# Output stage: head gates multiplied in first, the root's table loaded early, and the query columns repacked 256 wide for the U products

## The reference

```python
z = rmsnorm(x) * (1 + scale1) + shift1          # then one projection, three head groups
oa = gated_head_norm(hgrn2(...), ag, a_norm_g)  # heads of 64
ob = rglru(...) * gelu(by)
oc = gated_head_norm(delta(...), cz, dn_norm_g)
x = x + gt1 * (concat([oa, ob, oc]) @ w_out)
h = rmsnorm(x, norm2_g) * (1 + sc2) + sh2
q = h @ wq                                      # 8 heads of 128
# s1, s2 = the halves of q against 128 keys each; the 16 best pairs are the experts of a token
act = gelu(einsum('thkd,td->thk', u[idx], h))
x = x + gt2 * einsum('thk,thkd->td', softmax(scores) * act, v[idx])

def gated_head_norm(o, z, g):
    y = o * rsqrt(mean(o * o, axis=-1) + EPS)
    return y * g * silu(z)
```

## Time and profile before

| | |
|---|---|
| median of 3 runs | 2415.09 us (2414.5 to 2415.49) |
| the profiled execution | 2413.16 us, span 2411.3 us, mean granted clock 0.953 |
| PE matmuls busy | 2272.0 us (94%), 20740 instructions |
| PE weight loads busy | 2112.7 us (88%) |
| DVE, ACT, POOL busy | 1560.5 us (65%), 1271.9 us (53%), 1180.5 us (49%) |
| U products, PE L460 and L464 | 4096 and 2048 matmuls of 256 columns, mean 281 and 280 ns |
| V products, PE L2646 and L2650 | 4096 and 2048 matmuls of 256 columns, mean 279 and 279 ns |
| a high part on ACT, 128 x 512 (L408) | mean 632 ns |

### The profile page before, as it was taken

The page is one execution under the profiler, slowest core; times in us unless marked ns, Lnnn a source line. Parts: engine busy times, 40 slices in busy tenths (PEclk is TensorE's granted clock), DMA queues, the critical chain, the costliest instruction groups (busy, mean ns, idle before and its releaser), DMA issues. The chain is left out here.

```text
span 2411.3 us, 59210 instructions
## 1 busy us (share of the span) xinstructions
PE 2272.0 (94%) x20740; PEld 2112.7 (88%) x20740; DVE 1560.5 (65%) x3155; ACT 1271.9 (53%) x2423; POOL 1180.5 (49%) x1064
## 2 busy tenths in 40 slices
PE   6987989999999999999979789899999999999998
PEld 4954879999998799999979357899999987999997
DVE  2737756973224968888657466589532268787885
ACT  2540245558556955555536203455675578555554
POOL 0005147884445746566300232688744466565661
PEclk7988889999999999999979679999999999999999
DMA  6466024555553079889534740445555511898992
GB/s 251 169 253 228 3 107 156 176 187 190 189 184 112 0 258 313 282 302 312 178 143 165 264 166 12 142 166 175 191 192 184 189 54 69 283 311 278 312 309 102
DMA packets 123825, 455.58 MB, mean 189 GB/s; under 512 B 13744, under 2 KB 14256, under 8 KB 122544
## 3 DMA queue, kind: packets, MB, share of 16 engines
q1 hardware_dynamic: 105264, 386.80, 44.3%
q0 software_dynamic: 18432, 67.12, 9.9%
HBM read 449.37 MB, written 4.49 MB: 188 GB/s over the span
## 5 line engine op out<-in xcount | busy, mean ns | idle before, releaser
L415 POOL TENSOR_TENSOR parts<-ring,parts 128x512 fp32r<-128x512 f32 x358 | 462.6, 1294 | 283.3 <-ACT parts L408 266.3
L408 ACT ACTIVATE parts<-ring 128x512 fp32r<-128x512 f32 x616 | 386.7, 632 | 369.2 <-PE ps_u L464 285.4
L460 PE MATMUL ps_u<-h_parts,parts 128*128 128x256 f32 x4096 | 569.4, 281 | 1.0 <-ACT parts L408 0.6
L2646 PE MATMUL ps_y<-act_parts,parts 128*128 128x256 f32 x4096 | 562.5, 279 | 0.0
L460 PEld LDWEIGHTS ps_u<-h_parts,parts 128*128 128x128 f32 x4096 | 518.2, 189 | 3.5 <-ACT parts L408 2.2
L2646 PEld LDWEIGHTS ps_y<-act_parts,parts 128*128 128x128 f32 x4096 | 515.0, 188 | 0.9 <-ACT parts L2586 0.7
L415 DVE TENSOR_TENSOR parts<-ring,parts 128x512 fp32r<-128x512 f32 x258 | 178.6, 695 | 390.0 <-ACT parts L408 366.0
L2695 POOL TENSOR_TENSOR act_parts<-big,act_parts 128x256 fp32r<-128x256 f32 x256 | 245.5, 959 | 305.7 <-ACT act_parts L2675 305.7
L464 PE MATMUL ps_u<-h_parts,parts 128*128 128x256 f32 x2048 | 324.1, 280 | 1.1 <-DVE parts L415 0.8
L2650 PE MATMUL ps_y<-act_parts,parts 128*128 128x256 f32 x2048 | 322.2, 279 | 0.0
L464 PEld LDWEIGHTS ps_u<-h_parts,parts 128*128 128x128 f32 x2048 | 279.2, 190 | 2.0 <-DVE parts L415 1.2
(11 more groups left out here) (394 smaller groups left out, 3109.0 us busy)
## 6 DMA issues: line engine op xcount, KB each, us to landing
ring<-in_stream SPq DMA_DIRECT2D x522, 512.0 KB, 3.8
more_ring<-in_stream SPq DMA_DIRECT2D x126, 512.0 KB, 3.5
extra_ring<-in_stream SPq DMA_DIRECT2D x48, 512.0 KB, 5.4
big<-in_stream SPq DMA_DIRECT2D x16, 512.0 KB, 12.0
out_state_out<-big SPq DMA_DIRECT2D x2, 1440.0 KB, 8.4
big<-in_state SPq DMA_DIRECT2D x2, 1280.0 KB, 10.7
big<-in_mixc SPq DMA_DIRECT2D x2, 1024.0 KB, 8.2
big<-in_spots SPq DMA_DIRECT2D x2, 1024.0 KB, 5.4
```

The lines of the kernel that those rows point to most:

```text
L408: eng.activation(m.parts[:, q % PARTS, 0, :], half_tile(m, t, half), ACT.Copy).then_inc(s["hi_ready"], 1)
L415: eng.tensor_tensor(m.parts[:, q % PARTS, 1, :], half_tile(m, t, half), m.parts[:, q % PARTS, 0, :].bitcast(F32), ALU.subtract).then_inc(m ...
L460: pe.matmul(out, hi[:, k, :], hr[:, side, kk, 0:tokens], start=(kk + side == 0), stop=False)
L2646: pe.matmul(ps[:, half * KD // 2 + k, :], hi[:, k, :], act_parts[:, j % AHEAD, side, :], start=False, stop=False)
```

## The change

Three edits, all in the output stage.

1. The gates are multiplied into `m.mixed` before the norm: two instructions for tiles 0 and 1, one of 128 x 864 for tiles 5 to 7. The norm's `scalar_tensor_tensor` is then the last step of a column.
2. A Sqrt of one element makes ScalarE load the root's table before the sums are there. For that the order on ScalarE and VectorE changes: only column part 0 stands ahead of the root, the others behind it.
3. `h_parts` is now interleaved, column by column, hi and lo side by side. For the U products the first 256 tokens of the second norm's output are split once more, into a `narrow` view on the same memory: column k at 512k, its low part 256 further on. Column k may be written when query product 2k+1 has been done, since it covers the wide columns up to k alone.

```diff
@@ output_block, ScalarE
-            for i in range(READY):
-                high(i)
-                mixed_high(i)
+            high(0)
+            mixed_high(0)
+            act.activation(tmp[:, 0, 0:1], m.eps, ACT.Sqrt).then_inc(s["root_loaded"], 1)
             act.wait_ge(s["sums_ready"], 1)
             act.activation(norm, ps[0:12, 4, 0:NT], ACT.Sqrt, bias=m.eps[0:12, :], scale=1.0 / HD).then_inc(s["root_ready"], 1)
+            for i in range(1, READY):
+                mixed_high(i)
+                high(i)
...
+            def again_high(k):
+                act.wait_ge(s["parts_used"], OUT_Q + 2 * k + 2)
+                act.activation(narrow[:, 0, k, :], m.h[:, k, 0:NP], ACT.Copy).then_inc(s["u_hi"], 1)
+
+            again_high(0)
+            again_high(1)
             for q in range(OUT_Q + KD, ALL_Q):
                 high(q)
+                if q % 2:
+                    again_high((q - OUT_Q - 5) // 2)
+            again_high(KD - 2)
+            again_high(KD - 1)
             for h in COPY_ACT:
                 wait_head(act, h)
@@ output_block, VectorE
-            for i in range(READY):
-                mixed_low(i)
+            mixed_low(0)
+            v.wait_ge(s["squares_ready"], 2)
+            for n, t in enumerate(tiles[:2]):
+                v.tensor_tensor(m.mixed[:, t, :], m.mixed[:, t, :], m.zact[:, 6 + t, :], ALU.mult).then_inc(s["gated"], 1)
             v.wait_ge(s["root_ready"], 1)
             v.reciprocal(norm, norm).then_inc(s["inverse"], 1)
...
+            v.tensor_tensor(m.mixed[:, 5:8, :], m.mixed[:, 5:8, :], m.zact[:, 11:14, :], ALU.mult).then_inc(s["gated"], 1)
+            for i in range(1, READY):
+                mixed_low(i)
+            v.wait_ge(s["gated"], 3)
             for n, t in enumerate(tiles):
...
                 v.scalar_tensor_tensor(m.mixed[:, t, :], m.mixed[:, t, :], g, ps[:, spread_bank[n], 0:NT],
-                                       ALU.mult, ALU.mult).then_inc(s["spread_read"], 1)
+                                       ALU.mult, ALU.mult).then_inc(s["normed"], 1)
                 if n:
-                    gated(n - 1)
-                if n > 1:
-                    mixed_low(READY + n - 2)
-            gated(len(tiles) - 1)
-            mixed_low(KD - 2)
+                    mixed_low(READY + n - 1)
             mixed_low(KD - 1)
...
+            for k in range(KD):
+                v.wait_ge(s["u_hi"], k + 1)
+                v.tensor_tensor(narrow[:, 1, k, :], m.h[:, k, 0:NP], narrow[:, 0, k, :].bitcast(F32), ALU.subtract).then_inc(
+                    s["u_lo"], 1)
             for h in COPY_DVE:
@@ build
-            with nc.sbuf_tensor("h_parts", [P, 2, KD, NT], F32R) as hr:
-                output_block(nc, m, l, hr, stream, small_out, state_out)
-                experts_block(nc, m, l, hr, stream, spots_in)
+            with nc.sbuf_tensor("h_parts", [P, KD * 2 * NT], F32R) as parts:
+                wide = parts.rearrange("p (k s t) -> p s k t", s=2, t=NT)
+                narrow = parts[:, 0:KD * 2 * NP].rearrange("p (k s t) -> p s k t", s=2, t=NP)
+                output_block(nc, m, l, wide, narrow, stream, small_out, state_out)
+                experts_block(nc, m, l, narrow, stream, spots_in)
```

More of the change, by code:

```diff
@@ L1979, in _, with output_block @@
             new_state(4)
-def output_block(nc, m, l, hr, stream, small_out, state_out):
-    names = ("step squares_ready sums_ready root_ready inverse spread spread_read normed out_ready x_ready squares2 sums2 "
-             "root2 h_ready hi_ready lo_ready parts_used mix_hi mix_lo h_hi h_lo query_ready query_out outs_saved states_saved")
+def output_block(nc, m, l, hr, narrow, stream, small_out, state_out):
+    names = ("step squares_ready sums_ready root_ready inverse spread normed out_ready x_ready squares2 sums2 "
+             "root2 h_ready hi_ready lo_ready parts_used mix_hi mix_lo h_hi h_lo u_hi u_lo gated root_loaded query_ready query_out outs_saved states_saved")
     tiles = (0, 1, 5, 6, 7)
@@ L2091, in column_low @@
                 v.tensor_tensor(hr[:, 1, k, :], m.h[:, k, :], hr[:, 0, k, :].bitcast(F32), ALU.subtract).then_inc(s["h_lo"], 1)
-            for i in range(READY):
-                mixed_low(i)
+            mixed_low(0)
+            v.wait_ge(s["squares_ready"], 2)
+            for n, t in enumerate(tiles[:2]):
+                v.tensor_tensor(m.mixed[:, t, :], m.mixed[:, t, :], m.zact[:, 6 + t, :], ALU.mult).then_inc(s["gated"], 1)
             v.wait_ge(s["root_ready"], 1)
             v.reciprocal(norm, norm).then_inc(s["inverse"], 1)
-            def gated(n):
-                t = tiles[n]
-                gate = m.zact[:, 6 + t, :] if t < 2 else m.zact[:, 11 + t - 5, :]
-                v.wait_ge(s["spread_read"], n + 1)
-                v.tensor_tensor(m.mixed[:, t, :], m.mixed[:, t, :], gate, ALU.mult).then_inc(s["normed"], 1)
+            v.tensor_tensor(m.mixed[:, 5:8, :], m.mixed[:, 5:8, :], m.zact[:, 11:14, :], ALU.mult).then_inc(s["gated"], 1)
+            for i in range(1, READY):
+                mixed_low(i)
+            v.wait_ge(s["gated"], 3)
             for n, t in enumerate(tiles):
@@ L2134, in _ @@
                 v.tensor_copy(m.query[:, h, :], ps[:, h, 0:NT])
-            v.wait_ge(s["h_lo"], KD)
+            v.wait_ge(s["u_lo"], KD)
         @block.tensor
@@ L2179, in _ @@
             out_product(0, 2, 3)
-            pe.wait_ge(s["spread_read"], 1)
+            pe.wait_ge(s["normed"], 1)
             spread_norm(4)
```

## The result

The changed kernel took 2424.38 us (median of 6 runs, 2422.72 to 2425.98) against 2414.8 us for the kernel before, measured beside it: ratio 1.0037, 95% interval 1.0023 to 1.0050. The forecast was 2427. The profiled execution took 2425.98 us (span 2424.1, mean granted clock 0.948), against a span of 2411.3 before.

A forecast was written before the change was run, and what follows sets the result against it. TensorE's matmuls, busy 94% of the span, bound the kernel. Head +2.0 and +1.5, its clock +2.6, ends +3.7, one fall there +1.8, U 0: +11.6 us, on the 2415.09 median about 2427; range 2413 to 2431.

The forecast's parts named there:

- order of the head, both layers: Output stage's head: late low part 1 delays product 1 and the spreads; +2.0 us layer 0, +1.5 layer 1.
- clock in the head, layer 0, layer 1: Behind the head's longer stop the clock falls in both layers; layer 0 as before, 0, layer 1 +2.6 us.
- longer stop at the ends: Output stage's end: the last column's split and copies follow the last query product; +1.85 us a layer, +3.7 in all.
- clock behind the ends: After the longer stop before the scores, one clock fall in the two layers; +1.8 us, bounds 0 and 5.
- U's beat: U stage: halves stay at 1.413 us despite the repack; 0, bounds -6.9 and +3.4 us.
- GpSimd in the head: GpSimd works beside the reciprocal, then the gate holds it up; a reciprocal blocking it was the +3.2 us high end, dropped.
- The rule of the Trainium skill: VectorE instructions with at most one SBUF input, outside two-port modes, do not contend with GpSimd; removed the head's +3.2 us.
- The note on cachelines: U's reads: only stride inside a read costs; both layouts are read contiguously, so the repack gains nothing.
- rival 2: U halves go to 1.400 us but clock falls come as forecast; +4.7 us, 2419.8; chance 16%.

The follow-up runs named there:

- g2: e1 with 9 fp32 matmuls to an unused bank between output products 0 and 1, both layers; 2418.7 us, ratio 1.0011.
- h1: e2 with 3 fp32 matmuls in TensorE's stop at the output stage's end, on a bank already copied out; 2415.2 us, ratio 0.9993.
- e2: The kernel before with only the repacking (second split into 256-wide columns), without the head edits; 2414.91 us, ratio 1.0002.
- g1: e1 with VectorE's wide gate moved behind low parts 1 and 2; 2417.74 us, ratio 1.0010.
- e1: The kernel before with only the head edits (gates first, early root table), without the repacking; 2422.09 us, ratio 1.0029.
- e3: The kernel before with h_parts interleaved, high and low parts side by side, 288 wide each, no second split; 2413.04 us, ratio 0.9987.
- g4: e3's layout plus another head order that puts nothing ahead of low part 1; 2404.77 us, ratio 0.9951 against the kernel before.
- g3: The changed kernel with its packed query columns 2176 bytes apart instead of 2048; 2426.13 us in one run.
- h2: g4 with e3's layout undone: g4's head order on the kernel before's layout; 2408.57 us, ratio 0.9972.
- e4: The repack alone, packed 256 wide, columns 1024 bytes apart, but high and low parts 9216 bytes apart; 2417.45 us, ratio 1.0011.

## Why the prediction came out, term by term

The time was right within 3 us, but two terms were wrong by about as much as each other, with opposite signs. That they cancelled is luck; the range held because both lay within the bounds that were kept.

| term | predicted | measured | from |
|---|---|---|---|
| order of the head, both layers | +2.0, +1.5 | +1.7, +1.7 | g2 less 0.93, against 74.55 |
| clock in the head, layer 0, layer 1 | 0, +2.6 | +1.2, +4.4 | after less 1.8 (end) less 76.25; layer 0 also less the 2.7 it lost before |
| longer stop at the ends | +3.7 | +3.6 | 3.13 against 1.35, twice |
| clock behind the ends | +1.8 | +2.8 | h1 against e2, scores to U's end |
| U's beat | 0 | -4.9 | -2.1 in the table, less the 2.8 above |
| sum | +11.6 | +10.5 | medians: +9.6 |

The last two measured terms can be told apart in the changed kernel itself. From the scores' start to the ninth U half it took 14.96 and 14.93 us against 13.45 and 13.40 before, +3.0 us, which is the clock at the ends; from there to the last half 354.85 and 354.95 against 357.62 and 357.27, -5.1 us, which is the beat.

**Right: the stops.** The head's reading held nearly to the instruction: the reciprocal was forecast to end 5.6 us after the head's first matmul and ended at 5.52, the wide gate was put at 1.05 us and took 0.98, product 1 was put at 8.2 us and came at 7.92. g1 shows the wide gate's part in it: with that one line moved, 2 of the 3.2 us go away. The spreads, put 2.0 us later, are so by order alone: in g2, where the clock held, they start 10.75 us after the head's first matmul, less 0.93 for the fill 9.82, against 7.78. In the changed kernel they came 3.3 us later, the rest being the clock. The end's stop was put at 1.85 us longer, and was 1.78; e1 and e3, without the second split, have the old stop.

**Right in size, wrong in mechanism: GpSimd in the head.** I had it run one low part beside the reciprocal and be held up by the gate in its second. What the rows show is one instruction that began at 317.97 and ended only at 321.08, after 3.115 us instead of 1.29: it stood still through the reciprocal (to 319.05) and the gate (to 319.96). In g4, with the reciprocal and then a low part of 0.38 us beside it, GpSimd's part took 2.48 us. So the reciprocal did hold it: behind the last instruction that held it GpSimd's part took another 1.12 and 1.13 us in the two cases, nearly the whole of its 1.29. (The profile's times on GpSimd are rough, but the 3.12 recur in all eight heads of after, e1, g2 and g3, and 2.47 to 2.48 in all four of g4 and h2.) I had priced that at +3.2 us because I counted two of GpSimd's instructions ahead of low part 1; there was one. The rule of the Trainium skill that I cited (SBUF — State Buffer, "Who interferes with whom") did not hold for this reciprocal of 12 x 288, and the measurement decides.

**Wrong: the U beat (predicted 0, measured about -4.9).** The step that failed is "1.400 and 1.413 are two beats that one layout can have, and U's layout is not shown to be the cause of its beat". The first half stands, since in the changed kernel and in e4 the early stretch reads 1.413. The second does not: of before, e1, g1, g2, h2 and g3, whose columns stand 1152 or 2176 bytes apart, no long stretch reads 1.400; of after, e2, e3, e4, g4 and h1 the two later ones all do. V's rows showed both beats, and I let the slower one outvote the faster. What I could have asked is which layouts ever show 1.400 at all, and U's old one never did. The note on cachelines of the Trainium skill (SBUF — State Buffer, "Door 1: The DMA port swizzle"), by which I had the repacking gain nothing, did not foresee this either: both layouts are contiguous inside a read, and the beats differ.

**Wrong: the clock (predicted +4.4, measured +8.4).** I gave the two ends one fall; there were two, in all four kernels with a 3.13 us stop (8 ends of 8), while none of the ends with 1.35 us fell. In the heads I forecast a fall in both layers, which came, but counted layer 0 as no worse than before; with two falls inside each head it was 1.2 us worse, and layer 1 lost 4.4 where I had 2.6. What brings the second fall, with no stop ahead of it, is open; e1's layer 1 had only one and lost 1.4. g2 and h1, which change only what TensorE does in the stop, show that the clock's share is real: without it the same orders are 1.5 to 3.4 us shorter wherever it fell (h1 up to the ninth U half), but for e1's layer 1 (0.5, or 1.4 without the fill's own 0.93).

So what happened is rival 2's mechanism with more falls than it had, not the forecast's. Rival 2's 2419.8 missed by 4.6 us, the forecast's 2427 by 2.6. The split that e1 and e2 give (about +6.5 and 0, some 3 us short of the whole) points the same way: the repacking bought as much as it cost, and the head edits were the loss.

Left open: whether the multiple of 256 bytes is the rule for the beat (the old layout with its columns padded to 1280 bytes would test it most directly; it was not run), why the early 40 halves of U keep another beat, why e1 and e2 together cost less than the changed kernel, and why the same stop of 1.32 us in the head was followed by a fall in 7 of the 10 heads of before, e2, e3, e4 and h1, and in 3 of these not.

## What to carry to other kernels

When work is moved ahead on an engine, look first at what the moved instructions now stand in front of: here the reciprocal came 2 us earlier and the low part behind it 3 us later, and TensorE waited for the low part first. Every stop of 3.07 or 3.13 us in these two places cost its length and then once more some 1 to 4 us for the clock, while those of 1.35 us before the scores never did; so a change that lengthened one by 1.8 us had to bring more than 3 to pay. Before copying operands into a better layout, try giving them that layout where they are first written.

## What was not expected of the hardware

The beat of 12 matmuls of 256 columns depends on how far apart the moving operand's columns stand: 1.413 us at 1152 and 2176 bytes (1.420 in some stretches), 1.400 at 1024, 2048 and 2304 in most, at a granted clock of 1.00. A VectorE reciprocal with one SBUF input of 12 x 288 held back GpSimd's two-input tensor_tensor, by at least 0.8 us in g4 (2.48 us, less 1.29 and the 0.38 of the low part). The rows of g4, VectorE and then GpSimd:

```profile
314.80 1.94 DVE L2100 RECIPROCAL big<-big 12x288 f32<-12x288 f32 x1
316.67 0.38 DVE L2090 TENSOR_TENSOR h_parts<-big,h_parts 128x288 fp32r<-128x288 f32 x1
```

```profile
315.70 2.48 POOL L2082 TENSOR_TENSOR parts<-ring,parts 128x512 fp32r<-128x512 f32 x1 [1.21 <-ACT parts L2027]
```

It began 0.97 us before the low part did; unhindered it would have had 0.32 us left by then. This is not so for every reciprocal: one of 128 x 16 in h2 fell wholly inside a GpSimd part that had begun first, and that part took no longer than 1.29 us. Whether the width or the order makes the difference is not shown.

```profile
570.40 1.29 POOL L415 TENSOR_TENSOR parts<-ring,parts 128x512 fp32r<-128x512 f32 x1 [1.50 <-ACT parts L408]
...
570.56 0.25 DVE L2430 RECIPROCAL rms<-rms 128x16 f32<-128x16 f32 x1
```

In the other direction a two-input gate of 128 x 864 took 2.13 us beside GpSimd (g1) and 0.98 us when it came in first (the changed kernel).
